# Constant-block matmuls at the start of eleven stages of a three-layer network kernel

## The reference

```
layer 0:  h = rms_norm(x) * (1 + scale) + shift        # per token norm, per feature modulation
          x = x + g1 * (concat(neighbourhood_attention, mlstm)(h @ w_in) @ w_out)
          x = x + g2 * (square(relu(h2 @ w1)) @ w2)     # width 4096
layer 1:  the same frame; the mixer is an RWKV-like recurrence: projections k, v, r of mixed tokens,
          low-rank terms, a chunked recurrence, a group norm, a gate, then an output projection; then an MLP
block 2:  projection w_in (6688 columns), short convolutions, a gated delta rule and a state space
          recurrence, an output projection of 2048 rows; then 32 experts, 4 per token, of clamped SwiGLU
result:   rmsnorm(x) * final_g
```

## Time and profile before

| | us |
|---|---|
| median of 3 runs | 3341.05 (3336.45 to 3348.66) |
| the profiled execution, its own time | 3339.89 |
| its span, first to last instruction | 3338.1 |
| TensorE busy in it | 2914.3 (87%) |
| mean granted TensorE clock | 0.939 of full |

### The profile page before, as it was taken

The page is one execution under the profiler, slowest core; times in us unless marked ns, Lnnn a source line. Parts: engine busy times, 40 slices in busy tenths (PEclk is TensorE's granted clock), DMA queues, the critical chain, the costliest instruction groups (busy, mean ns, idle before and its releaser), DMA issues. The chain is left out here.

```text
span 3338.1 us, 78969 instructions
## 1 busy us (share of the span) xinstructions
PE 2914.3 (87%) x34998; PEld 1942.6 (58%) x34998; DVE 1343.1 (40%) x2053; ACT 933.6 (28%) x1598; POOL 306.6 (9%) x253
## 2 busy tenths in 40 slices
PE   7988899999987788877899997786999998998995
PEld 4865568887665666664898786674333333333332
DVE  3355643334854554653555675464111110111013
ACT  3124532323323343331444553332111100110010
POOL 0021200000401231130000002202000000000000
PEclk8989899999988999998899998897999999999997
DMA  7272322223142100104454431077999999999995
GB/s 261 77 257 88 139 76 101 79 98 129 51 182 81 54 23 23 54 4 162 176 185 171 153 127 54 16 270 276 363 421 422 421 422 421 421 421 421 422 421 219
DMA packets 195159, 681.01 MB, mean 204 GB/s; under 512 B 25617, under 2 KB 40465, under 8 KB 145505
## 3 DMA queue, kind: packets, MB, share of 16 engines
q1 hardware_dynamic: 175424, 651.93, 50.1%
q10 hardware_dynamic: 18336, 21.21, 1.8%
q0 software_dynamic: 1152, 4.19, 0.3%
HBM read 651.86 MB, written 25.43 MB: 203 GB/s over the span
## 5 line engine op out<-in xcount | busy, mean ns | idle before, releaser
L3937 PE MATMUL experts_psum_gu<-ring,experts_x 128*32 128x512 f32 x3840 | 430.9, 597 | 35.1 <-DMA ring<-in_w_gu 35.1
L4059 DVE TENSOR_SCALAR experts_gate<-experts_psum_gu 128x768 f32<-128x768 f32 (+1 forms) x32 | 26.4, 825 | 853.1 <-PE experts_psum_gu L3937 853.1
L3937 PEld LDWEIGHTS experts_psum_gu<-ring,experts_x 128*32 128x32 f32 x3840 | 111.7, 110 | 336.2 <-issue 241.0
L3966 PE MATMUL experts_psum_down<-down_weights,experts_hiddenT 128*32 128x256 f32 x4096 | 231.6, 381 | 16.0 <-DMA down_weights<-in_w_down 12.9
L3966 PEld LDWEIGHTS experts_psum_down<-down_weights,experts_hiddenT 128*32 128x32 f32 x4096 | 127.6, 110 | 129.0 <-DMA down_weights<-in_w_down 32.8
L4003 ACT ACTIVATE experts_sigmoid<-experts_gate 128x768 f32<-128x768 f32 (+1 forms) x32 | 23.6, 739 | 586.0 <-DVE experts_gate L4059 586.0
L982 PE MATMUL mlp_psum_bank<-mlp_x_high,mlp_w_high 128*128 128x512 f32 (+1 forms) x512 | 176.2, 344 | 8.6 <-DVE xT_rounded L469 5.3
L315 DVE TENSOR_TENSOR ring_rounded<-ring,mlp_w_high 128x1024 fp32r<-128x1024 f32 x128 | 156.8, 1225 | 44.2 <-ACT mlp_w_high L310 44.2
L982 PE MATMUL mlp_psum_bank<-xT_rounded,mlp_w_high 128*128 128x512 f32 (+1 forms) x512 | 173.8, 339 | 0.0
L992 PE MATMUL mlp_psum_bank<-mlp_hidden_high,mlp_w_high 128*128 128x512 f32 (+1 forms) x512 | 172.4, 337 | 1.2 <-ACT mlp_relu L928 1.2
L982 PE MATMUL mlp_psum_bank<-mlp_x_high,ring_rounded 128*128 128x512 f32 (+1 forms) x512 | 173.3, 338 | 0.0
(11 more groups left out here) (763 smaller groups left out, 5911.6 us busy)
## 6 DMA issues: line engine op xcount, KB each, us to landing
ring<-in_w_gu SPq DMA_DIRECT2D x192, 1024.0 KB, 25.9
down_weights<-in_w_down SPq DMA_DIRECT2D x96, 1024.0 KB, 27.4
ring<-in_ada_w SPq DMA_DIRECT2D x72, 1024.0 KB, 10.8
ring<-in_mlp_w SPq DMA_DIRECT2D x64, 1024.0 KB, 7.0
xT<-in_w_gu SPq DMA_DIRECT2D x64, 1024.0 KB, 26.0
ring<-in_w_in SPq DMA_DIRECT2D x24, 1024.0 KB, 6.6
spare_unit<-in_w_down SPq DMA_DIRECT2D x16, 1024.0 KB, 30.0
x<-in_w_down SPq DMA_DIRECT2D x16, 1024.0 KB, 26.7
```

What stands on the lines that cost most here:

```text
L3937: mm = nc.tensor.matmul(pg[32 * j:32 * j + 32, gr, :, :], x, strip(w, j), start=False, stop=(u == U - 1))
L3966: mm = nc.tensor.matmul(pd[32 * c:32 * c + 32, gr, :], hidT[:, a, gr, GROUP * v:GROUP * v + GROUP], w[:, a, C * c:C * c + C], start=(v == ...
L4059: v.tensor_scalar(G, pg[:, 0:groups, 0, :], SWI_LIMIT, None, ALU.min).then_inc(s_gt, 1)
```

## The change

A new function issues `n` matmuls of the 128 by 128 block of ones by 256 columns of constants, in float32, into a part of a bank that the stage's next product overwrites. They wait for nothing, and nobody waits for them. Two stand ahead of each `spread` and four behind it (six stages); five stand ahead of the first products of `gemm_feat`, `gd_conv` and `gemm_rows`, and in `rw_readout` between the first two steps and the wait for the loads (five stages). With `gemm_tok`, `mlp` and `gemm_feat` used twice each, that is 61 matmuls in eleven stages.

```
+def keep_busy(g, dst, n):
+    for _ in range(n):
+        g.nc.tensor.matmul(dst, blk(g, C_ONE), g.const[:, 0:256], start=True, stop=True)

 gemm_tok, mlp (banks), rw_project, router (pl):
+                keep_busy(g, banks[:, 0, 0:256], 2)
                 xs.spread(pe)
+                keep_busy(g, banks[:, 0, 0:256], 4)
                 ring.take(pe)

 gemm_feat, gd_conv, gemm_rows:
+                keep_busy(g, banks[:, 0, 0:256], 5)
                 for ...:                 # the first products

 rw_readout:
                 m.step(pe, 0)
                 m.step(pe, 1)
+                keep_busy(g, ps[:, 0, 0:256], 5)
                 fetch.wait(pe)
```

More of the change, by code:

```diff
@@ L1787, in lora @@
                             mm.then_inc(s_hp, 1)
+                keep_busy(g, pl[:, 0, 0:256], 2)
                 h.spread(pe)
+                keep_busy(g, pl[:, 0, 0:256], 4)
                 lora(0, g.xT)
```

## The result

The kernel with the change takes 3317.75 us (median of 10 runs, 3310.38 to 3331.18), the kernel before, measured beside it, 3341.29 us (10 runs, 3333.09 to 3348.66). The ratio is 0.9929 with a 95% interval of 0.9912 to 0.9947: by the ratio 23.7 us faster, give or take 6 (the medians differ by 23.5). The forecast was 3321 us in a range of 3313 to 3338. The profiled execution took 3318.79 us, its span 3317.0, which is 21.1 us less than before.

The account below looks back on a forecast made before the run. Bound: non-overlapping stages, with TensorE at half clock after pauses where the stage waits for it. Gains 8.2 + 2.2 + 9.75 = 20.2 us off the profiled 3339.9 give 3319.7, about 3321 us as median; range 3313 to 3338.

Parts of the forecast that it names:

- What bounds the kernel: All stages: they don't overlap, so savings add; half clock after pauses costs only where the stage waits for TensorE.
- What an added matmul costs: Each added matmul: 0.85 us at half clock, 0.43 at full, plus one exposed load; five take 4.6 or 2.3 us.
- Five ahead of the products, 8.2 us: `about`, `rwout`, `gdconv`, `mixout`: five fit the pauses, products start at full clock; gain 8.2 us, between 0 and 9.0.
- Two ahead of the spread, loss of 4.6 us: Six norm stages: two added matmuls delay the spread and VectorE behind it; 5.75 us at half clock, 0.8 at full, 4.6 taken.
- Four behind the spread, gain of 6.8 us: Norm stages: full-clock products return 1.6 us in `projAB`, 1.6 in `proj2`, 2.1 in `mlp1`, 1.5 in `router`; sum 6.8.
- the products should start at full clock: Norm stages: two, spread and four are dense work for 5 to 7 us, longer than the longest wait for a rise.
- Five in `rwread`, 9.75 us: `rwread`: five fill the 2.76 us pause and the clock stays full, saving half of 19.50 us; at worst loss 1.8.
- The rival of this term: `rwread`: the gate matmuls lose the full clock, so the stage gives only 0 to 1 us; 3331 us in all, chance 0.26.
- The gates don't hold the clock: `rwread`: gate matmuls fall to half clock, giving 0 to 1 us; total gain 10.5, so 3331 us; chance 0.26.
- The product stages are paced by others: `about`, `rwout`, `mixout`: ScalarE and VectorE hold TensorE; four stages give 3 us, total near 3, so 3338 us; chance 0.14.
- Slower: Begin of each stage: added matmuls run at half clock and raise nothing; sum 19 us, about 3357 us; chance 0.10.
- under 33 us: Whole kernel: estimate of what all clock ramps together are worth, from the skill page's below 1% of a typical span.

Follow-up runs that it names:

- the one with nothing but the split wait: Against the kernel before: in `rwread` TensorE waits only for the loads its gates read, issued first, and no matmul is added; 3327.8 us, ratio 0.9974.
- the second run of the change: The unaltered change measured again on another chip, against the kernel before; 3313.8 us (6 runs), ratio 0.9928.
- the second experiment: Against the kernel after, only the five added matmuls ahead of products in `about`, `rwout`, `gdconv` and `mixout` remain; 3327.5 us, ratio 0.9984 to the kernel before.
- the first experiment: Against the kernel after, only the five added matmuls in `rwread` remain; 3327.3 us, ratio 0.9981 to the kernel before.
- The three parts alone: Kernels keeping one part of the change each: only the five in `rwread` 3327.3 us, only the fives ahead of products 3327.5, only twos and fours 3333.2.
- the doubled fives: Against the kernel after, ten in place of five added matmuls ahead of the products of `about`, `rwout`, `gdconv`, `mixout`; 3320.4 us, ratio 0.9950.

## Why the prediction was right, by its own steps

**What bounds the kernel: right.** The half-clock stretches were the loss, they follow the pauses, and the stages add up: 22.2 us in the touched ones make 21.1 of the whole. The experiment with two columns shows that no side effect of the added instructions does it, and the one with nothing but the split wait shows the gates at full clock, and the stage 12 us shorter, with no instruction added. Two readings of the rows were off. The pauses of 2.84 to 3.20 us count from the stage's begin; TensorE had been idle longer, 4.00 to 5.04 us ahead of the four first products. And "the longest wait for a rise here" was 6.20 us only with the 13.64 and 19.50 us of the earlier trace rows left aside.

**What an added matmul costs: right.** The rows of L482 of the kernel after (shortest, median and longest of a record in ns):

```profile
L482 PE MATMUL about_psum_bank<-const x10: 379/379/454, 401.0 to 403.0; 128*128 128x256 f32 x10
L482 PE MATMUL rwread_psum_gate<-const x10: 379/379/462, 1545.0 to 1547.0; 128*128 128x256 f32 x10
L482 PE MATMUL rwout_psum_bank<-const x10: 379/631/763, 1584.6 to 1588.1; 128*128 128x256 f32 x10
```

Five take 2.40 us at full clock from start to end (2.3 predicted), 3.87 in `rwout`, where the clock was half at first, and 4.61 in the second run of the change, where it was half all through (4.6 predicted).

**Five ahead of the products, 8.2 us: right in three of four stages.** The stages give 1.9 + 1.6 + 3.2 + 1.3 = 8.0. In `about` and `mixout` this is the predicted half of the stretch, 2.0 and 1.4. In `rwout` it is less than the predicted 2.7, for the reason that the prediction named: the pause was entered with the clock down (0.57 over the fives), and the first product came 0.6 us late. That `gdconv` gave 3.2 is not shown: with nothing added there it took 143.5 to 143.9 us in three kernels' profiles and 147.4 and 148.1 in two, and with the fives 144.1 to 146.2. The other three repeat. Over all profiles, one of each kernel (that with 2 columns counted as without), `about` took 56.1 to 56.3 us without its five and 54.2 with them (once 55.0), `mixout` 53.5 to 54.6 and 52.2 in all eight, `rwout` 32.2 to 32.6 and 29.9 to 32.0. With `gdconv` left out the term is 4.8 us, and the second experiment's 5.3 us (1.0 to 9.7) can't tell the two apart.

**Two ahead of the spread, loss of 4.6 us: mechanism right, sum too large.** The begin of `mlp0` in the kernel after, TensorE and then VectorE:

```profile
455.19 2.05 PE L482 MATMUL mlp_psum_bank<-const 128*128 128x256 f32 x4 [2.04 <-PEq L156]
457.03 1.92 PE L442 MATMUL mlp_psum_bank<-mlp_inverse_diag,const 128*128 128x512 f32 x2
458.74 3.11 PE L482 MATMUL mlp_psum_bank<-const 128*128 128x256 f32 x8
461.93 0.47 PE L991 MATMUL mlp_psum_bank<-mlp_x_high,mlp_w_high 128*128 128x512 f32 x1
```

```profile
459.06 1.66 DVE L451 SCALAR_TENSOR_TENSOR xT<-x,mlp_scale,mlp_psum_bank 128x256 f32<-128x256 f32 x4 [1.49 <-PE mlp_psum_bank L442]
```

VectorE's first product with the spread starts 3.87 us after the begin in place of 2.93 (458.51 - 455.58), so 0.94 later; 1.0 was predicted for half clock. TensorE's first products came later by 0.9 in `projAB`, 0.9 in `mlp0`, 0.6 in `rwproj`, 0.7 in `proj2` and 0.1 or less in `mlp1` and `router`, where the clock was full at the stage's begin: 3.2 us, not 4.6. The diagonal was ready at 455.88, and the spread started only at 457.03, when the added two were all but done (their entry ends at 457.24; neighbours overlap by 0.2 us in these rows). The Trainium skill (TensorE: Matmul & The Clock Gate, Part 3, "The mechanism") states that matmuls start and end in strict order; the trace agrees, since the spread did not pass the two.

**Four behind the spread, gain of 6.8 us.** Net of the delay the six stages give 0.3 - 1.0 + 1.8 + 0.3 + 1.2 + 2.7 = 5.3 us in the profile, where 2.2 were predicted; the experiment with these alone measures a loss of 0.7 us (gain of 4.0 to loss of 5.3). The interval holds the predicted 2.2, the profile is one execution, and neither tells more. Over all profiles the six stages are some 3.8 us shorter in the mean of the seven kernels with twos and fours than in that of the five without, but `router` alone ranges from 60.7 to 63.9 with them and from 62.6 to 64.3 without. Single terms were off. `mlp1` was to give 2.1 and gave 0.3. Here the step "the products should start at full clock" did not carry far enough: the clock fell again behind the first products (0.72 over the 6.20 us). In five other profiles, where it was at 0.99 or 1.00 over the first 8 us, the stage took 196.5 to 197.1 us and so gave 0.6 to 1.2; the rest of the 2.1 VectorE, busy all 6.20 us, may have held, but no run separates that. `rwproj` was to give nothing and gave 1.8, but not at its begin, where VectorE is busy 45.54 of 45.73 us; the saving lies in its last third, where before a spell at half clock (3.4 us from 983.6) followed a wait of 2.18 us. The second run of the change gave 1.0 there. It stays open whether that spell is chance. `router` gave 2.7 against 1.5: its first 13.64 us are at a mean of 0.71 in place of 0.50, with a fall in the middle that the six matmuls at the begin did not prevent. In the second run of the change the stage gave 0.3 us only.

**Five in `rwread`, 9.75 us: right where they reach the end of the wait.** The stage is 8.9 us shorter, the ring load 10.3 us sooner, every gate at half its time. What was open, whether the gates hold a full clock when they did not raise a low one, is settled: in the kernel before with the split wait the gates followed the steps with no added matmul between, and they stayed at 1.10 to 1.13 us each. The step lacked one thing: the pause's length varies, and the five do not always reach its end. The rival of this term, 0 to 1 us for the stage, is what the profile of the first experiment shows, for another reason than the one given for it: not the gates lost the clock, the pause did.

**The rivals.** "The gates don't hold the clock" falls with the window of the gates at 1.00 over 8.39 us. "The product stages are paced by others" falls in `about`, `rwout` and `mixout` (all TensorE-busy at full clock, with 1.8 times the matmuls) and holds in `mlp0`; in `mlp1` it is not separated from the clock. "Slower" falls with the clocks; the doubled fives show that its price is real once the matmuls stick out of the pause. The change took off 0.71% of the time. The Trainium skill (same page, Part 1, "What's actually happening") states that ramps cost less than 1% of a typical kernel's span; the 0.71% does not test this, since it is the touched stages alone. The mean clocks of 0.939 and 0.951 mean 409 us at half clock before and 327 after, with TensorE busy in 280 and 226 of them, so this trace leaves room for far more than 1%: half of 280 us, an estimate from above since TensorE is not always what is waited for, is 140 us or 4.2%. The "under 33 us" of the prediction's estimate was not borne out by anything here.

**What stays open.** The three parts alone give 6.3 + 5.3 - 0.7 = 11 us (3 to 19 with their intervals), the change 23.7 (18 to 29). Whether a part works better in company (with the five of `rwread`, say, failing less often), or luck took one side, the runs don't tell. That the forecast came within 4 us of the median (20.2 us off predicted, 23.7 measured) is in part luck: terms that were off by 1 to 2 us each (`mlp1`, `rwproj`, `router`, `rwout`) went both ways, and the profile of the second run of the change has 17.4 us in the touched stages, 2.7 of them in `gdconv`, where a gain is not shown. Nor do the runs say why untouched stages differ between profiles by up to 11 us (`rwkv` 491 to 502, `ssd` 117 to 124).

## What to carry to other kernels

Look for stretches at half clock behind short pauses of TensorE, and take only those where TensorE is what the stage waits for; a constant matmul into a bank that is overwritten next, as many as fit the pause and no more, gave back half of such a stretch in `about` and `mixout`. First ask whether the pause itself must be: a wait for loads that the next matmuls don't read was worth 12 us of a 56.6 us stage when it was split (5 to 12 us of the whole time by the runs), without any added work. Fill with matmuls that have work in them (256 columns here; those of 2 columns did nothing), and put none ahead of a small matmul that another engine waits for.

## What the runs showed of the hardware that was not expected

A pause can be paid for after it has ended. In the kernel with the five in `rwread` only, the clock read 1.00 through a pause of 1.95 us and then 0.51 over the 15.71 us of dense gates behind it; without the five (all else as in the change) 1.00 through 3.07 us and then 0.52. A look at the clock in the pause alone would have found nothing there. In the kernel before it fell inside the pause (0.82 over 2.76 us), so the gates have to be looked at in either case.

The gate matmuls (128 rows and 32 rows in turn, float32, engine busy all the time) are neutral in both directions for as long as they last here: they held a full clock for 8.4 us at 1.00, and left a low one low for 16 us (1547.74 to 1563.84 in the kernel before).

Ten records of 2 columns in the same pause did not keep the clock for the gates: it read 1.00 through the 2.87 us left of the pause, and the gates ran at 2.07 or 2.08 us each, as before.
